# Where the 184 weight panels of the second block are split into two halves: GpSimd in place of ScalarE and VectorE

## What is computed

```python
for l in range(DEPTH):                       # DEPTH = 2
    h_lat = _rms(x, norm_w[l]) * (1.0 + scale) + shift
    h_ctx = _rms(ctx, norm_w[l]) * (1.0 + scale_c) + shift_c
    if l % 2 == 0:
        y_lat, y_ctx = _ab_mixer(h_lat, h_ctx, ...)
    else:
        y_lat, y_ctx = _c_mixer(h_lat, h_ctx, ...)
    x = x + gate * y_lat
```

## Time and profile before

| | |
|---|---|
| median of 3 runs | 2892.94 us (2892.57 to 2893.07) |
| the profiled execution, span | 2892.0 us |
| TensorE busy | 2531.0 us, 88% |
| VectorE busy | 1879.6 us, 65% |
| ScalarE busy | 1134.6 us, 39% |
| GpSimd busy | 86.7 us, 3% |
| `low` L1629, whole kernel | 490 instructions, 596.5 us, 184 of them in the second block |
| `high` L1178, whole kernel | 490 instructions, 515.1 us, 184 of them in the second block |

### The profile page before, as it was taken

How to read it: one execution, slowest core, us unless ns; L and a number is a source line. 1 busy time by engine, 2 the same in 40 slices (tenths; PEclk the granted TensorE clock), 3 DMA queues, 4 the chain that set the end, 5 groups by cost and what they waited for, 6 DMA issues and landing times.

```text
span 2892.0 us, 41541 instructions
## 1 busy us (share of the span) xinstructions
PE 2531.0 (88%) x14924; PEld 2180.8 (75%) x14924; DVE 1879.6 (65%) x3624; ACT 1134.6 (39%) x1637; POOL 86.7 (3%) x140
## 2 busy tenths in 40 slices
PE   6999759998999769996889889999959799999978
PEld 6998458997998458994667667777737588888868
DVE  5775867777775867774444433544543498898984
ACT  3333333333333433333443432333222355555553
POOL 0000000000000000002111100110000000000000
PEclk9998969998999869998999978999979899999998
DMA  6553005545554005544232411121102122222212
GB/s 234 207 187 139 22 8 188 211 168 199 206 182 148 13 15 195 210 168 81 51 57 59 58 37 59 44 73 58 37 22 87 58 88 80 80 79 73 73 65 95
DMA packets 81042, 297.49 MB, mean 103 GB/s; under 512 B 9792, under 2 KB 10304, under 8 KB 80192
## 3 DMA queue, kind: packets, MB, share of 16 engines
q1 hardware_dynamic: 77760, 284.20, 27.8%
q0 software_dynamic: 2048, 4.20, 2.6%
q10 hardware_dynamic: 1152, 8.03, 0.7%
HBM read 295.34 MB, written 1.05 MB: 102 GB/s over the span
## 4 chain that ended last, share of the span: by engine, by line
PE 65%; DVE 24%; ACT 6%; issue 3%; DMA 1%; POOL 0%; DVEq 0%; ACTq 0%; SPq 0%; POOLq 0%; another core or an unknown queue 0%
PE ps L644 52%; DVE work L1744 3%; DVE wsplit L1629 3%; PE ps L1017 2%; PE ps L663 1%; DVE work L2217 1%; DVE work L1674 1%; ACT wsplit L1178 1%; DVE work L2187 1%; DVE work L2179 1%; DVE work L2238 1%; PE ps L884 1%; PE ps L903 1%; ACT work L1570 1%; PE ps L892 1%
## 5 line engine op out<-in xcount | busy, mean ns | idle before, releaser
L644 PE MATMUL ps<-hsplit,wsplit 128*128 128x256 f32 (+1 forms) x9456 | 1598.3, 329 | 79.8 <-DVE hsplit L1817 22.4
L644 PEld LDWEIGHTS ps<-hsplit,wsplit 128*128 128x128 f32 x9456 | 1393.4, 196 | 238.5 <-issue 45.6
L1629 DVE TENSOR_TENSOR wsplit<-ring,wsplit 128x1024 fp32r<-128x1024 f32 x490 | 596.5, 1223 | 359.9 <-ACT wsplit L1178 344.8
L1178 ACT ACTIVATE wsplit<-ring 128x1024 fp32r<-128x1024 f32 x490 | 515.1, 1056 | 763.1 <-PE ps L644 729.8
L644 PE MATMUL ps<-fsplit,wsplit 128*128 128x256 f32 x2112 | 278.7, 290 | 15.5 <-DVE wsplit L1629 9.4
L644 PEld LDWEIGHTS ps<-fsplit,wsplit 128*128 128x128 f32 x2112 | 269.8, 199 | 16.6 <-issue 10.2
L1674 DVE SCALAR_TENSOR_TENSOR work<-ring,cs,work 128x128 f32<-128x128 f32 x672 | 206.1, 348 | 9.0
L663 PE MATMUL ps<-work,ones 128*128 128x256 f32 x192 | 59.0, 475 | 53.0 <-ACT work L1184 53.0
L1201 ACT ACTIVATE work<-ps 128x256 f32<-128x256 f32 x88 | 33.7, 383 | 163.3 <-PE ps L644 163.3
L1744 DVE SCALAR_TENSOR_TENSOR work<-work,vec 128x256 f32<-128x256 f32 x240 | 97.6, 477 | 0.0
L1652 DVE TENSOR_TENSOR work<-ps,work 128x256 f32<-128x256 f32 x88 | 37.3, 424 | 88.1 <-ACT work L1201 88.1
(11 more groups left out here) (296 smaller groups left out, 2531.7 us busy)
## 6 DMA issues: line engine op xcount, KB each, us to landing
ring<-panels SPq DMA_DIRECT2D x538, 512.0 KB, 4.2
work<-latent_weights ACTq DMA_DIRECT2D x2, 2304.0 KB, 11.1
work<-rpb POOLq DMA_DIRECT2D x64, 64.0 KB, 6.4
cst<-constants ACTq DMA_DIRECT2D x1, 1904.0 KB, 9.6
xT<-x SPq DMA_DIRECT2D x1, 1024.0 KB, 10.2
cT<-ctx ACTq DMA_DIRECT2D x1, 1024.0 KB, 4.7
out<-xT SPq DMA_DIRECT2D x1, 1024.0 KB, 3.9
vec<-vectors ACTq DMA_DIRECT2D x2, 87.5 KB, 4.6
```

Of the source, the lines that this page charges most:

```text
L644: ins = mm(out_, w(a), x(b), start=start and n == 0, stop=stop and n == 2, **kw)
L1178: af(wsplit[:, split_slot(name, n), 0, :], ring[:, p % slots, :], ACT.Copy).then_inc(high_ready, 1)
L1629: tt(parts[:, 1, :], ring[:, p % slots, :], parts[:, 0, :].bitcast(fp32), ALU.subtract)\
```

## The change

GpSimd gets a function `split` that makes both halves of a panel, one instruction after the other, and calls it for all 184 panels of the second block. Every `high` and `low` of the second block is taken out of ScalarE's and VectorE's programs; the first block keeps its own. GpSimd's loops are written out, and the bias loads, the bias masks and the B masks stand between the splits.

```diff
@@ scalar: every high of A, B, OAB, C, OC is removed, for instance
-                high("C", 0, nx[0] + 1, nx[1])
                 act.wait_ge(panels_used, n0 + 5)
...
@@ vector: every low of A, B, OAB, C, OC is removed, for instance
                 ins.then_inc(c_ak_ready, 1)
-                low("C", 0, nx[0] + 1, nx[1])
                 if before:
                     c_output(h - 1, 1 - par)
...
@@ gpsimd
+            def split(name, n):
+
+                p, slots = SEC[name].where(n), SEC[name].slots
+                pool.wait_ge(loaded[p % slots], loads_of(name, 0, p))
+                pool.wait_ge(panels_used, split_count(name, 0, n - depth(name)) + START)
+                parts = wsplit[:, split_slot(name, n), :, :]
+                nc.gpsimd.tensor_copy(parts[:, 0, :], ring[:, p % slots, :]).then_inc(high_ready, 1)
+                pool.wait_ge(high_ready, split_count(name, 0, n))
+                nc.gpsimd.tensor_tensor(parts[:, 1, :], ring[:, p % slots, :], parts[:, 0, :].bitcast(fp32), ALU.subtract)\
+                    .then_inc(low_ready, 1)
...
+            split("A", 0)
+            split("A", 1)
+            pool.wait_ge(x_in_place, LAYERS + 1)
+            bias_load(0, 0)
+            split("A", 2)
+            split("A", 3)
+            bias_mask(0, 0)
+            bias_load(1, 1)
+            split("A", 4)
+            split("A", 5)
+            bias_mask(1, 1)
+            split("A", 6)
+            split("A", 7)
+            for c in range(2, 8):
+                split("A", 4 * c)
+                pool.wait_ge(a_out_ready, 2 * c - 2)
+                bias_load(c, c % 2)
+                split("A", 4 * c + 1)
+                split("A", 4 * c + 2)
+                bias_mask(c, c % 2)
+                split("A", 4 * c + 3)
...
+            def b_head(h, more):
+
+                n0 = 10 * h
+                for n in range(6, 12 if more else 10):
+                    split("B", n0 + n)
+                b_masks(h, 0)
+                if more:
+                    for n in (12, 13):
+                        split("B", n0 + n)
+                b_masks(h, 1)
+                if more:
+                    for n in (14, 15):
+                        split("B", n0 + n)
+
+            for n in range(6):
+                split("B", n)
+            for h in range(ML_HEADS):
+                b_head(h, h + 1 < ML_HEADS)
+            for n in range(16):
+                split("OAB", n)
+            for n in range(80):
+                split("C", n)
+            for n in range(16):
+                split("OC", n)
```

More of the change, by code:

```diff
@@ L1349, in _ @@
             act.wait_ge(ctx_loaded, 32)
-            norm(9, cT, before=lambda part: (h_ready, 72), between=("A", 0))
+            norm(9, cT, before=lambda part: (h_ready, 72))
             high_norm(1, 0, 1)
@@ L1509, in _ @@
             y_highs(0)
-            for n in range(2, 10):
-                high("OAB", 0, n)
             act.wait_ge(panels_used, used_by("OAB", 0, 8))
             y_highs(1)
-            for n in range(10, 16):
-                high("OAB", 0, n)
             act.wait_ge(oab_ready, 16)
-            norm(10, xT, between=("C", 0))
+            norm(10, xT)
             high_norm(2, 1, 0)
@@ L2004, in _ @@
             tt(b_M[0:4, :, :], g_F[0:4, :, :], b_R[0:4, :, :], ALU.add).then_inc(g_rows_stage, 1)
-            for n in range(3, 6):
-                low("B", 0, n)
             dve.wait_ge(g_products_done, 3)
@@ L2018, in b_head @@
                     .then_inc(b_rows_ready, 1)
-                for n in range(6, 8):
-                    low("B", 0, n, h * 2)
                 cos = cst[:, K_CB:K_CB + 512].rearrange("p (a t) -> p a t", a=2)
@@ L2077, in b_head @@
                 weights(0)
-                if more:
-                    for n in (12, 13):
-                        low("B", 0, n, h * 2)
                 dve.wait_ge(b_pv_done, h * 2 + 1)
@@ L2084, in b_head @@
                 normalise(0, (3, 4, 7))
-                if more:
-                    for n in (14, 15):
-                        low("B", 0, n, h * 2)
                 dve.wait_ge(b_pv_done, h * 2 + 2)
@@ L2119, in _ @@
             y_lows(0)
-            for n in range(2, 10):
-                low("OAB", 0, n)
             y_lows(1)
             for m in range(KD):
-                if m < 6:
-                    low("OAB", 0, 10 + m)
                 dve.wait_ge(panels_used, used_by("OAB", 0, m + 9))
@@ L2131, in _ @@
             norm2(10, xT, 1, 0)
-            for n in range(2):
-                low("C", 0, n)
             norm2(11, cT, 1, 1)
@@ L2195, in c_head @@
                 tt(c_kh[:, :, :], c_kk[:, :, T:2 * T], c_kh[:, :, :], ALU.mult).then_inc(c_kh_ready, 1)
-                if more:
-                    low("C", 0, nx[0] + 2, nx[1])
                 if before:
@@ L2210, in c_head @@
                     .then_inc(c_q_ready, 1)
-                if more:
-                    low("C", 0, nx[0] + 3, nx[1])
                 dve.wait_ge(c_ek_ready, h + 1)
@@ L2271, in _ @@
             for m in range(KD):
-                for n in (2 * m + 2, 2 * m + 3):
-                    if n < 16:
-                        low("OC", 0, n)
                 dve.wait_ge(panels_used, used_by("OC", 0, 2 * m + 2))
@@ new lines, in b_masks @@
+            def b_masks(h, d):
+                for st in range(4):
+                    pool.wait_ge(b_prod_ready, h * 8 + (4 * d + st + 1))
+                    G.did(nc.gpsimd.tensor_tensor(pool_fence[:, :], eps_b[:, :], eps_b[:, :], ALU.add))
+                    G.need()
+                    p = b_p[:, b_cols[st]]
+                    p = p if st < 2 else p[:, T:2 * T]
+                    sign = 1 if d == 0 else -1
+                    nc.gpsimd.affine_select(out=p, in_=p, compare_op=ALU.is_ge, fill=0.0,
+                                            base=-sign * (st % 2) * 128, pattern=[[sign, T]],
+                                            channel_multiplier=-sign).then_inc(b_p_ready, 1)
```

62 lines of the change are left out of this document (2 added, 60 removed).

## The result

The changed kernel takes **3045.26 us** (median of four runs, 3043.20 to 3050.15) against 2892.76 for the kernel before beside it: a ratio of **1.0532** (95% interval 1.0517 to 1.0547), 152 us slower. The forecast was 3018. The profiled execution took 3043.2 us, with a span of 3041.5 against 2892.0.

The account below looks back on a forecast made before the run. In C both TensorE and VectorE were taken as nearly full, so VectorE's waits for GpSimd cost there. C 100, OC 10, OAB 2, B 10, A 3 make +125 on 2892.0 us: 3018, range 2965 to 3085, reaching 2915 to 3125.

Parts of the forecast that it names:

- C: Stage of 16 heads, TensorE and VectorE nearly full: head from 33.8 to 40.5 us, +100 us over fifteen heads.
- No exclusion where VectorE has two SBUF inputs: Rival: long waits only for forms like L1951; C gains 24 us, OC loses 10; 2879 us, faster; chance 0.1.
- half the exclusion: Rival: VectorE wins most turns, GpSimd works in its gaps and PSUM operations; C +8, 2921 us; chance 0.2.
- VectorE's instructions are back to back there, so the two engines alternate: C head, scans and ladders: each short VectorE instruction can wait for a 2.39 us GpSimd one; 14.8 us added.
- dear copy: Rival: GpSimd's copy costs 2.39 us, adding 100 us in C and 19 in OC; 3137 us; chance 0.1.
- OAB: Stage with panels every 5.44 us: splits stay hidden, only y_lows(1) meets one; +2 us.
- OC: Stage with panels every 2.88 us: GpSimd needs 3.6 and becomes the pace; +10 us.
- 25.7 + 14.8 = 40.5: C head: VectorE's own remaining work plus its waits for GpSimd, in us; 6.7 more than now.
- TensorE, at 32 us, then has slack: C head: TensorE's 32 us of work fits inside the lengthened head of 40.5 us.
- A: Attention heads: +0.5 us for each of six pairs, +3 us in all, bounds -5 and +12.
- Later in the pair L1951 is ready before it is needed: Stage A: after the pair's start, delay to VectorE's L1951 does not hold TensorE; part of A's +3 us.
- B: Matrix recurrence heads: next head's first two splits fall on L2094 and L2096, 3.4 us three times; +10 us, bounds 0 and 21.

Follow-up runs that it names:

- d1: Kernel before plus useless GpSimd copy and subtraction in scratch SBUF for each of 78 C panels, which nobody waits for: 3079.39 us, ratio 1.0644.
- d2: Kernel before plus useless GpSimd work in C that only writes SBUF, four memsets of 1024 columns per panel: 2904.57 us, ratio 1.0045.
- g1: Kernel before with the last two subtractions of each C head on GpSimd, held back until the third ladder ends: 2869.25 us, ratio 0.9919.
- g2: Kernel before with the last two subtractions of each C head on GpSimd, without a wait for the third ladder's end: 2896.4 us, ratio 1.0011.
- b1: Changed kernel, but in B GpSimd splits the next head's first two panels only after VectorE has finished the head: 3037.37 us, ratio 1.0503.
- t1: Changed kernel with A's first two splits moved behind the wait for the end of the first block: 3040.10 us, ratio 1.0506.
- p1: Changed kernel plus twelve idle matmuls on TensorE in each C head, ahead of its wait for the ladder's result: 3038.05 us, ratio 1.0501.
- e4: Kernel before with only C's subtractions moved to GpSimd, the copies staying on ScalarE: 2917.92 us, ratio 1.0086.
- e2: Kernel before with only C's splits, copies and subtractions, moved to GpSimd: 3008.83 us, ratio 1.040.
- e1: Changed kernel with C's copies and subtractions given back to ScalarE and VectorE: 2928.80 us, ratio 1.0123.
- g3: Kernel before with g1's edit, and GpSimd also splitting OAB's panels 2 to 15 and C's first two: 2869.70 us, ratio 0.9916.

## Why the prediction was right, and where it was off

**Right: the sign, the place and the mechanism.** Exclusion between GpSimd's reads and VectorE's operations on SBUF, C as the stage that pays, PSUM readers untouched, short additions waiting for whole GpSimd instructions. d1 against d2 shows it is the reads; g1 against g2, b1 and t1 show that the same work costs little or nothing in another place. *No exclusion where VectorE has two SBUF inputs* (2879) is out by the ladders alone, *half the exclusion* (2921) by a C that lost 120 us where it allowed 8.

**Wrong in one ladder of three.** "VectorE's instructions are back to back there, so the two engines alternate" holds for the scans and the third ladder and fails for the second. The prediction had L2179, L2187 and L2217 all stretched to about 0.7 us; they came out at 0.67, 0.42 and 1.12 (means over C). In the second ladder VectorE wins every turn, as the rival *half the exclusion* has it.

**The copy's price, right.** Free copies took 1.04 us where 1.05 was taken, so the rival of a dear copy is out. Where VectorE is waiting, in OAB:

```profile
2216.11 1.04 POOL L2217 CAST wsplit<-ring 128x1024 fp32r<-128x1024 f32 x1 [1.93 <-PE ps L644]
```

The estimate of 1.5 us from the Trainium skill, "GPSIMD Engine Reference", section 3.1, does not hold here; the measurement decides. The "some 60 us" beside it are too many by the prediction's own terms: 0.45 us more a copy, five copies in fifteen heads and fourteen in OC, is 40.

**C, right in kind, too small by 20 us** (+120 for +100). Of the step "25.7 + 14.8 = 40.5" the first number held. The waits, read as what VectorE is busy beyond the instructions' free durations, are 13.4 us instead of 14.8 (in the head above L2149 5.9, L2131 and L2140 2.2 each, L2116 2.0, the scan 0.8, small ones the rest), spread otherwise than sketched. The 25.7 us still contained 1.3 us of idle time; the head above has 3.3, so 25.7 + 13.3 + 2.0 = 41.0. What failed is "TensorE, at 32 us, then has slack": it can stand still for 7.3 us, but its clock falls, and VectorE then waits behind its matmuls. p1's heads at a clock of 1.00 take 39.4 us, so the clock accounts for 1.5 us. Another 0.5 us of idle time is not the clock's: the low that stood between the eviction and the selects is gone, and VectorE reaches TensorE's result sooner. e4, at a clock of 1.00 throughout, waits 0.9 us there, p1's heads at 1.00 likewise, the undisturbed heads before 0.5.

That the head came so near 40.5 is in part luck: 1.4 us too much of waiting stand against 1.5 us of clock that the prediction left out.

The measured head is 0.6 us over the forecast. Another 0.5 comes from the base: the window of the earlier trace rows was one of the longer heads, and the mean of the kernel before is 33.23 us. The last of the fifteen steps grew by 10.2 us (41.8 to 52.0) where it was counted at 6.7. 14 x 1.1 + 3.5 = 19 of the 20 us.

**A term that was missing, 7 us.** The prediction began at the second block. A0's panel lands at 1299.2 us, GpSimd waits for nothing else, and the first two splits fall on the end of the first block, on fourteen products of two tensors with a norm behind them. The products grew by 5.7 us and the norm's matmuls, at the lower clock, by 3.1; the products had begun 1.7 us earlier. t1 removes both: in its trace the second block's first VectorE instruction comes at 1311.3 us, 8.8 earlier than in the changed kernel. Of these 8.8 us 7.3 are left at A's first matmul and 5 in the time.

**A, too small.** +3 was taken with a bound of +12; it was about +10. The step "Later in the pair L1951 is ready before it is needed" failed. The counterpart of the earlier trace rows:

```profile
L1917 DVE TENSOR_SCALAR work<-work x64: 352/486/2637, 1384.1 to 1734.2; 128x512 f32<-128x512 f32 x32, 128x256 f32<-128x256 f32 x32
```

The median is the old one, the tail is not: all 64 take 50.0 us in place of 30.6, and 20 of them more than 0.6 us, where 2 did. TensorE's idle time ahead of L892, which waits for them, before and after:

```profile
L892 PE MATMUL ps<-cst,work 128*128 128x128 f32 x192 | 36.1, 302 | 42.1 <-DVE work L1951 41.5
L892 PE MATMUL ps<-cst,work 128*128 128x128 f32 x192 | 36.3, 303 | 54.2 <-DVE work L1917 53.4
```

These 12 us cover A's 10. L1917 reads only one tensor, in SBUF, so being held by GpSimd doesn't take two inputs. No run isolated A.

**B, right** (+10.2, and 8 returned by b1). At a head's end, VectorE, the counterpart of the earlier trace rows:

```profile
1986.32 2.45 DVE L2037 SCALAR_TENSOR_TENSOR work<-work 128x512 f32<-128x512 f32 x2 [5.96 <-ACT work L1475]
...
1988.92 3.12 DVE L2039 TENSOR_TENSOR work<-work 128x1024 f32 x1 [0.16 <-DVE work L2037]
```

1.0 + 1.9 = 2.9 us a head, where 3.4 was estimated, three times.

**OC, right**: GpSimd is the pace, and TensorE waits for it. The last panels of OC:

```profile
3023.01 1.04 POOL L2217 CAST wsplit<-ring 128x1024 fp32r<-128x1024 f32 x1
...
3026.48 1.04 POOL L2217 CAST wsplit<-ring 128x1024 fp32r<-128x1024 f32 x1
```

The pitch is 3.47 us where 3.6 was predicted, and OC's first output to its last takes 48.7 us instead of 38.0, +10.7. The last C head ahead of it is 3.8 us shorter than before, so the stretch shows +6.9; no run looked into that part.

**OAB, about right; the gain lies behind it.** Split further, the stretch of -3.2 us has +1.5 in OAB itself (from its first activations to its last output, where +2 was predicted), -0.8 in the norms, and -3.9 between C's first matmul and the first head (24.1 to 20.2 us). e2 and e4, where OAB is as before, have this lead-in at 20.6 and 20.2 us; e1 and g3, where ScalarE and VectorE make C's splits there (g3 all but the first two), at 23.7. So the gain comes with C's own first splits, taken from ScalarE and VectorE, and the prediction had no term for it. g3 moved OAB's, which brings nothing.

**The range.** The working gives two: 2965 to 3085, and 2915 to 3125 for what it reaches. Its own upper terms (+36 in C, +9 in A, +11 in B) end at 3074.

## What to carry to other kernels

Count GpSimd's reads of SBUF and VectorE's instructions with two SBUF inputs as the use of one resource, and look at its other forms on SBUF too (L1951, one input, was held for 2.31 us in the earlier trace rows). Where both are busy, work moved from the one to the other gives nothing back, and at 2.39 us against 1.22 it costs twice. GpSimd helps where VectorE reads PSUM or is idle, and a semaphore that holds it back until then decides the sign (g1 and g2, 27 us apart). Where the waits make TensorE stand still, add what its clock then costs (1.5 us a head here). When a queue is emptied of its old waits, look at what its first instructions now run beside, in the section ahead of the change too.

## What the runs showed of the hardware beside that

- The exclusion is by whole instructions, but not always by turns. In the third ladder GpSimd gets in after one VectorE instruction (held 0.05 to 0.22 us); in the second it is kept out to the ladder's end, in every head of the changed kernel and of e4 (there for 3.1 us or more), and VectorE keeps 0.42 us. A GpSimd subtraction costs a 0.42 us VectorE instruction 2.1 us and one of 0.69 us 2.2, so ladders of short ones lose most, where they lose. VectorE's scans and its form with a scalar and two tensors (L1642) are subject to it like a plain addition; the select with its mask in SBUF and its data in PSUM is not (0.445 us).
- Writing alone is not wholly free. d2 lost 11 us though VectorE's ladder kept its time: in 11 of its first 14 heads the granted clock of the last 5 us was 0.66, and those heads took 33.9 to 34.6 us against 33.1 for those that ended at 1.00. The kernel before ends three of its heads at 0.75 to 0.78, and TensorE's wait ahead of L1125 in a head is 1.84 us in d2 against 1.60. L1125 averages 319 ns in d2 against 286. Why the clock falls with memsets beside is open.
- A memset of 128x1024 took 0.95 us on GpSimd. A VectorE copy of 3 columns beside it took 0.38 us instead of 0.15, so small copies do wait for something even there.
